# A fused two-layer kernel: two gate products as seven half-size products inside the level loop, and eleven PSUM banks moved to ScalarE

## The reference

```python
proj = h @ w_in                     # among its columns: gate_logits, 3 * 1024 wide
o_mla = causal_block_attention(...)            # 8 heads
o_gla = rms_norm(gla_chunked(...), g_gla_out) * silu(r_gla)   # 4 heads, linear attention with decay
o_mem = softmax(q_m k_m / sqrt(64)) v_m        # 4 heads over 256 memory rows
gates = sigmoid(gate_logits + b_gate).reshape(B, S, 3, D_MODEL)
y = gates[..., 0, :] * o_mla + gates[..., 1, :] * o_gla + gates[..., 2, :] * o_mem
x = x + y @ w_o
```

## Time and profile before

| | |
|---|---|
| median of 3 runs | 945.3 us (945.02 to 945.59) |
| the profiled execution, its own time | 943.98 us |
| its span | 941.6 us, so 2.4 us lie around it |
| PE busy | 926.9 us, 98% of the span |
| DVE busy | 710.9 us, 76% |
| ACT busy | 226.1 us, 24% |
| POOL busy | 37.6 us, 4% |
| chain that ended last | PE 87%, DVE 10%, ACT 1%, issue 1% |
| granted TensorE clock | full in every slice |

### The profile page before, as it was taken

The page is one execution under the profiler, slowest core; times in us unless marked ns, Lnnn a source line. Parts: engine busy times, 40 slices in busy tenths (PEclk is TensorE's granted clock), DMA queues, the critical chain, the costliest instruction groups (busy, mean ns, idle before and its releaser), DMA issues.

```text
span 941.6 us, 12480 instructions
## 1 busy us (share of the span) xinstructions
PE 926.9 (98%) x4976; PEld 584.0 (62%) x4976; DVE 710.9 (76%) x1237; ACT 226.1 (24%) x454; POOL 37.6 (4%) x58
## 2 busy tenths in 40 slices
PE   7999999999999999999999999999999999999998
PEld 5954455945555459999844459547864444469544
DVE  4875965589968787967899854888978789674676
ACT  5314422232231232332200011311103212324110
POOL 0400000000003400000000001000000000000000
PEclk9999999999999999999999999999999999999999
DMA  9753431453525624344444437522424244231721
GB/s 329 241 186 123 146 134 45 179 180 107 184 90 139 214 94 166 123 164 180 179 179 178 176 110 234 183 102 90 179 90 178 108 160 179 90 135 46 264 93 45
DMA packets 51960, 141.77 MB, mean 151 GB/s; under 512 B 4320, under 2 KB 8320, under 8 KB 51648
## 3 DMA queue, kind: packets, MB, share of 16 engines
q1 hardware_dynamic: 49152, 134.55, 40.4%
q0 software_dynamic: 2144, 5.84, 2.6%
q10 hardware_dynamic: 608, 0.61, 0.2%
HBM read 138.89 MB, written 2.10 MB: 150 GB/s over the span
## 4 chain that ended last, share of the span: by engine, by line
PE 87%; DVE 10%; ACT 1%; issue 1%; DMA 0%; DVEq 0%; ACTq 0%
PE pair L2149 30%; PE pair L2234 21%; PE pair L2230 16%; DVE arena L1079 7%; PE pair L2496 6%; PE turned L2090 3%; PE score L2496 3%; PE turned L2496 1%; PE score L2589 1%; PE score L2335 1%; PE score L2336 1%; PE score L2658 1%; PE score L2241 0%; DVE ring L1079 0%; PE turned L2576 0%
## 5 line engine op out<-in xcount | busy, mean ns | idle before, releaser
L2149 PE MATMUL pair<-ring,hT 128*128 128x512 f32 (+2 forms) x512 | 214.0, 573 | 0.9 <-ACT hT L695 0.9
L1079 DVE TENSOR_TENSOR arena<-arena 128x256 f32<-128x256 f32 (+5 forms) x326 | 194.2, 610 | 17.0 <-PE score L2496 4.1
L2149 PEld LDWEIGHTS pair<-ring,hT 128*128 128x128 f32 x512 | 95.3, 190 | 102.9 <-issue 97.7
L2234 PE MATMUL pair<-ring,arena 128*128 128x512 f32 x192 | 85.8, 594 | 0.0
L2234 PE MATMUL pair<-ring,hT 128*128 128x512 f32 x184 | 83.6, 595 | 0.1
L2234 PE MATMUL pair<-arena 128*128 128x512 f32 x176 | 79.5, 593 | 0.0
L1079 DVE TENSOR_TENSOR arena<-pair,arena 128x512 f32<-128x512 f32 x60 | 42.2, 704 | 47.2 <-PE pair L2234 26.0
L1079 DVE TENSOR_TENSOR arena<-ring 128x2048 f32<-128x2048 f32 (+1 forms) x39 | 72.3, 1854 | 2.2 <-DMA ring<-in_w_ssm_out 0.9
L2149 PE MATMUL pair<-hT,ring 128*128 128x128 f32 (+1 forms) x448 | 72.6, 322 | 0.2 <-ACT hT L691 0.2
L2149 PEld LDWEIGHTS pair<-hT,ring 128*128 128x128 f32 x448 | 64.6, 191 | 6.8 <-ACT hT L691 1.0
L2230 PE MATMUL pair<-arena 128*128 128x128 f32 x544 | 64.0, 276 | 0.0
(11 more groups left out here) (260 smaller groups left out, 1019.2 us busy)
## 6 DMA issues: line engine op xcount, KB each, us to landing
ring<-in_w_in SPq DMA_DIRECT2D x33, 2048.0 KB, 8.3
ring<-in_w_up SPq DMA_DIRECT2D x8, 2048.0 KB, 8.5
ring<-in_w_down SPq DMA_DIRECT2D x8, 2048.0 KB, 7.8
ring<-in_w_o SPq DMA_DIRECT2D x4, 2048.0 KB, 7.8
ring<-in_w_mem_kv SPq DMA_DIRECT2D x2, 2048.0 KB, 7.7
ring<-in_w_glu SPq DMA_DIRECT2D x2, 2048.0 KB, 7.8
ring<-in_w_ssm_out SPq DMA_DIRECT2D x2, 2048.0 KB, 7.8
ring<-in_w_ukv SPq DMA_DIRECT2D x1, 2048.0 KB, 7.6
```

Of the source, the lines that this page charges most:

```text
L1079: return dve.tensor_tensor(o, a, b, op)
L2149: ins = pe.matmul(o_, s, m, start=a, stop=b)
L2234: ins = pe.matmul(h[bank_], rows[:, k, :], weights[:, k, :], start=not onto and k == 0, stop=k == 3, skip_group_check=True)
```

## The change

The product for gates 4 and 5 becomes a group of seven named `GU`, spread over passes 4 to 8 of the level loop: products 1 and 5, then 2 and 7, then 3, 6 and 4. Its row sums are GT's, used again (`ROWS`). Its T1, T3 and T2 stand at the end of DVE's passes 3, 4 and 5; z and T4 at the end of pass 6. Its result is put together after the loop. Eleven banks that DVE took out of PSUM go to ACT: levels 1, 2 and 8, memory attention's four values, and the four outs. The clearing of `amat` goes from DVE to POOL, the squares of `o_gla` from DVE to ACT, and `gate_gain` from passes 4 and 5 to behind the loop. In group 2, earlier, product 7 moves ahead of the wait for `k_rows`. In the second block a one-element exponential stands ahead of the attention's loop, and `group_copy(RA, 1)` goes behind the first `exps`. POOL clears `gains`, `masks` and `m0` after `mixer_out`.

```diff
-    j = [(f"gate{i}", "w_in", C_GATE + 512 * i, 512) for i in (4, 5, 2, 3)]
+    out += halves(GT, C_GATE) + halves(GU, C_GATE + 2 * DM)
+    j = [(f"gate{i}", "w_in", C_GATE + 512 * i, 512) for i in (2, 3)]
...
@@ TensorE @@
             pe.wait_ge(sem("k_rows"), 1)      # group_multiply(2, 7) now ahead of this
...
-                elif i < 7:
-                    fill(["gate4", "gate5"], i - 4, 2)
                 else:
-                    fill(["gate4", "gate5"], i - 1, 1)
+                    for q in ((1, 5), (2, 7), (3,), (6,), (4,))[i - 4]:
+                        group_multiply(GU, q)
...
@@ VectorE, level loop @@
-                if i in (4, 5):
-                    gate_gain(i - 4)
...
-                    attend("mem", i - 2, lambda t: om_mem[:, t, EV * (i - 2):EV * (i - 1)])
+                    mark(dve.reciprocal(st[:, 360 + 2 * h:362 + 2 * h], st[:, 350 + 2 * h:352 + 2 * h]), "mem_sum")
...
-                if i == 0:
-                    link(dve.memset(amat, 0.0))
...
+                if i == 3:
+                    group_t1(GU)
+                if i == 4:
+                    group_t3(GU)
+                if i == 5:
+                    group_t2(GU)
+                if i == 6:
+                    group_z(GU)
+                    group_t4(GU)
-            for n in range(4):
-                p = scored()
-                taken_score(dve.tensor_copy(og3[:, n // 2, 512 * (n % 2):512 * (n % 2) + 512], p[:, :]))
-            gate_take(3)
...
@@ ScalarE, level loop @@
+                if i == 4:
+                    group_copy(GU, 1)
+                    group_copy(GU, 5)
...
+                if 2 <= i < EH + 2:
+                    p = ready("values", h)
+                    act.wait_ge(sem("mem_sum"), h + 1)
+                    for t in range(TT):
+                        ins = act.activation(om_mem[:, t, EV * h:EV * h + EV], p[:, EV * t:EV * t + EV], ACT.Copy,
+                                             scale=st[:, 360 + 2 * h + t:361 + 2 * h + t])
...
@@ ScalarE, second block @@
+            act.activation(st[:, 397:398], st[:, 399:400], ACT.Exp)
             for s in range(DH // 2):
-                if s == 0:
-                    group_copy(RA, 1)
...
                 for h in (2 * s, 2 * s + 1):
                     exps("dil", h, ((0, 384, 0), (384, 384, 1)))
+                    if h == 0:
+                        group_copy(RA, 1)
```

More of the change, by code:

```diff
@@ L81, with linear_units, copied @@
 SCORES = 37
-RG, MV, GT, UP = 3, 4, 5, 6
+def linear_units():
+    units = []
+    for i in range(9):
+        units += [("scores", i)] * (i < EH) + [("values", i - 2)] * (2 <= i < EH + 2) + [("level", i)]
+    return units + [("out", n) for n in range(4)]
+LINEAR = {u: 2 * MH + n for n, u in enumerate(linear_units())}
+BY_ACT = [n for u, n in LINEAR.items() if u[0] in ("values", "out") or u in (("level", 1), ("level", 2), ("level", 8))]
+def copied(*u):
+    return BY_ACT.index(LINEAR[u]) + 1
+RG, MV, GT, GU, UP = 3, 4, 5, 6, 7
 DK = UP + 4
@@ L172 @@
     "score_ready": "TensorE: banks of scores, values or states", "score_taken": "those banks out of PSUM",
+    "score_copied": "ScalarE: those of linear attention that it takes itself", "amat_zero": "GpSimd: zeros around the products within a tile",
+    "mem_sum": "heads whose sums of memory attention are inverted", "o_squared": "ScalarE: squares of a tile of linear attention's output",
     "act_step": "ScalarE's own", "dve_step": "VectorE's own", "pool_step": "GpSimd's own",
@@ L579, in _ @@
                     pool.memset(kmT[1][0:64, 0:SEQ], 0.0).then_inc(sem("key_zero"), 1)
+                    pool.wait_ge(sem("key_zero"), 4)
+                    pool.wait_ge(sem("group_product"), product_at(MV, 6))
+                    pool.memset(amat, 0.0).then_inc(sem("amat_zero"), 1)
                 if n in (2, 3):
@@ L705, in group_copy @@
                     act.wait_ge(sem("second_out"), i)
-                if i >= DK and q == 1:
+                if (i >= DK or i == GU) and q == 1:
                     act.wait_ge(sem("last_out"), i)
@@ L869, in level_exp, with ready @@
                 act.activation(dec, dec, ACT.Exp, scale=1.0 / 16.0).then_inc(sem("level_exp"), 1)
+            am3 = amat.rearrange("p (b n) -> p b n", n=P)
+            og3 = o_gla.rearrange("p (t c) -> p t c", c=DM)
+            om_mem = o_mem.rearrange("p (t c) -> p t c", c=DM)
+            def ready(*u):
+                n = LINEAR[u]
+                act.wait_ge(sem("score_ready"), n + 1)
+                return bank["score"][n % 2]
             for i in range(9):
@@ L874, in _ @@
                     level_exp(i)
+                if i == 2:
+                    p = ready("level", 1)
+                    act.wait_ge(sem("amat_zero"), 1)
+                    act.activation(am3[0:64, :, 64:128], p[0:64, :].rearrange("p (b n) -> p b n", n=64),
+                                   ACT.Copy).then_inc(sem("score_copied"), 1)
+                if i == 3:
+                    src = ready("level", 2)[:, 0:256].rearrange("p (b n) -> p b n", n=32)
+                    act.activation(am3[0:32, :, 32:64], src[0:32], ACT.Copy)
+                    act.activation(am3[64:96, :, 96:128], src[64:96], ACT.Copy).then_inc(sem("score_copied"), 1)
                 if i < 2:
                     group_copy(GT, (1, 5)[i])
+                if i == 4:
+                    group_copy(GU, 1)
+                    group_copy(GU, 5)
                 if 1 <= i <= EH:
@@ L886, in _ @@
                 if i == 8:
-                    gate_sigmoid(2)
-            gate_sigmoid(3)
+                    act.activation(across, ready("level", 8)[:, :], ACT.Copy).then_inc(sem("score_copied"), 1)
+            for n in range(4):
+                act.activation(og3[:, n // 2, 512 * (n % 2):512 * (n % 2) + 512], ready("out", n)[:, :],
+                               ACT.Copy).then_inc(sem("score_copied"), 1)
+            for t in range(TT):
+                act.wait_ge(sem("score_copied"), copied("out", 2 * t + 1))
+                act.activation((junk, qdec)[t], og3[:, t, :], ACT.Square).then_inc(sem("o_squared"), 1)
+            act.wait_ge(sem("first_out"), GU + 1)
+            act.wait_ge(sem("second_out"), GU + 1)
+            act.wait_ge(sem("last_out"), GU + 1)
+            act.activation(gate_buf, gate_buf, ACT.Sigmoid).then_inc(sem("gate_sig"), 1)
             for t in range(TT):
@@ L1522, in _ @@
                 if 2 <= i < EH + 2:
-                    attend("mem", i - 2, lambda t: om_mem[:, t, EV * (i - 2):EV * (i - 1)])
-                p = scored()
[L1526 to L1534, removed]
+                    n_score[0] += 1
+                    h = i - 2
+                    dve.wait_ge(sem("mem_exp"), h + 1)
+                    mark(dve.reciprocal(st[:, 360 + 2 * h:362 + 2 * h], st[:, 350 + 2 * h:352 + 2 * h]), "mem_sum")
+                    h, (_, _, z, v), biased = group(GT)[0], temporaries(GT), ckv[:, 0:512]
+                if i in (1, 2, 8):
+                    n_score[0] += 1
+                    if i < 8:
+                        dve.wait_ge(sem("score_ready"), LINEAR["level", i] + 1)
                 else:
+                    p = scored()
                     k = i - 3 if i else 5
@@ L1584, in _ @@
             mark(tt(o_gla, o_gla, r_gla, ALU.mult), "mixer_out")
-            gate_apply(2, 2)
-            gate_apply(3, 3)
+            dve.wait_ge(sem("score_copied"), len(BY_ACT))
+            dve.wait_ge(sem("gate_sig"), 2)
+            link(tt(o_mem, o_mem, gate_buf, ALU.mult))
             link(tt(o_mla, o_mla, o_mem, ALU.add))
@@ L2073, in _ @@
             n_unit = {"turned": 0, "score": 0}
+            by_dve = lambda n: n - sum(m < n for m in BY_ACT)
             turned_at = {}
@@ L2079, in unit @@
                 n_unit[kind] += 1
-                if n >= 2:
-                    pe.wait_ge(sem(kind + "_taken"), n - 1)
+                if kind == "score" and n - 2 in BY_ACT:
+                    pe.wait_ge(sem("score_copied"), BY_ACT.index(n - 2) + 1)
+                elif n >= 2:
+                    pe.wait_ge(sem(kind + "_taken"), by_dve(n - 1) if kind == "score" else n - 1)
                 return bank[kind][n % 2]
@@ L2307, in _ @@
             group_multiply(2, 2)
+            group_multiply(2, 7)
             pe.wait_ge(sem("k_rows"), 1)
@@ L2412, in _ @@
             pe.wait_ge(sem("amat"), 4)
+            pe.wait_ge(sem("score_copied"), copied("level", 2))
             for n in range(4):
+                if n == 2:
+                    pe.wait_ge(sem("score_copied"), copied("level", 8))
                 b = unit("score")
```

63 lines of the change are left out of this document (34 added, 29 removed).

## The result

| | before | after |
|---|---|---|
| median of the shared runs | 945.02 us (944.53 to 945.59, 5 runs) | 950.06 us (948.67 to 951.86, 5 runs) |
| profiled execution | 943.98 us, span 941.6 | 950.06 us, span 948.2 |

The ratio is 1.0054, with a 95% interval of 1.0039 to 1.0068: the change costs about 5 us. The forecast was 949.1, range 946.0 to 951.0.

What follows compares the result with a forecast made beforehand. PE was taken to bound the kernel, made to wait by DVE's sums: loop +5.5, group 2 -0.45, dilated attention -1.1, sum +3.9, rounded +3.8, so 947.8 us profiled and 949.1 for the runs, range 946.0 to 951.0.

Steps and rivals of the forecast that it cites:

- group 2: Earlier group: product 7 fills PE's 0.43 us wait for `k_rows` before the transpositions; -0.45 us, bounds 0 and -0.6.
- passes 0 to 3: Level loop's start: DVE loses clearing and copies, so PE's gaps of 1.46 and 0.69 us go; -2.15 us.
- pass 4: Level loop: product 5 waits for T1 behind DVE's chain of level 3, PE idles 2.8 us; 12.6 against 9.93, +2.7.
- pass 5: Level loop: the same chain, ending in T3, hangs on level 4, so the wait is paid again; 12.15 against 9.48, +2.7.
- passes 6 to 8: Level loop's end: product 6 waits 4.3 us for T2, product 4 for T4; 19.4 against 16.5, +2.9.
- outs, and up to `y`: Behind level 8: ACT takes level 8 instead of DVE, -0.45; DVE's lateness for `y` goes, -0.2.
- dilated attention: Second block: with the table loaded early and exponentials ahead of the copy, PE's wait for head 0 goes; -1.1 us.
- The waits: Level loop: PE idle 2.8 us each before products 5 and 7, 4.3 before 6, 2.3 before 4, ended by DVE sums.
- The clock's case: Rival: the 4.3 us wait halves PE's clock, product 6 takes 3.4 us more, 2.3 hidden; 950.2 to 953.6, chance 0.12.
- Half of it: Rival: DVE's chain is shorter than before's, each waiting pass 0.7 us less; +1.8, 947.1 us, chance 0.12.
- ScalarE was not late: Rival: ACT's added work in pass 4 delays the decays of level 5 by up to 2 us; 951, chance 0.06.
- the hidden case: Rival: PE never waits for T1 to T4, as DVE's gaps hide the sums; -7.8, 937.5 us, chance 0.09.

Runs made afterwards that it cites:

- e4: Before with only the one-element exponential ahead of the dilated attention and RA's product 1 copied behind head 0's exponentials; 942.89 us, ratio 0.9984 to before.
- e8: After with only T2, T4 and z made ahead of the level's taking, T1 and T3 left behind the levels; 943.76 us, ratio 0.9992 to before.
- e2: After with only T1 and T3 moved ahead of the level's taking, T2, z and T4 left in place; 942.94 us, ratio 0.9981 to before.
- e3: After with useless matmuls in PE's waits before products 5, 7 and 6, none before product 4; 949.35 us, ratio 1.0049 to before.
- e1: After with the same instructions, but all of DVE's sums of GU ahead of the level's taking; 936.50 us, ratio 0.9918 to before.
- e7: After with useless matmuls in all four of PE's waits, before products 5, 7, 6 and 4; 947.45 us, ratio 1.0031 to before.

## Why the prediction was right

Each step in the two profiled executions, from end to end of the same PE rows (after less before, us):

| step | forecast | measured | from |
|---|---|---|---|
| group 2 | -0.45 | -0.66 | first scores -1.15, of which -0.5 stood there already at 112 us |
| passes 0 to 3 | -2.15 | -2.28 | level 3 starts at 248.55 for 251.98, less the -1.15 |
| pass 4 | +2.7 | +2.8 | 12.7 for 9.93 |
| pass 5 | +2.7 | +4.3 | 13.8 for 9.48 |
| passes 6 to 8 | +2.9 | +2.95 | 19.46 for 16.51 |
| outs, and up to `y` | -0.65 | -0.8 | 29.4 for 30.15 |
| the loop | +5.5 | +7.0 | |
| dilated attention | -1.1 | -1.15 | |

The steps come to +5.2 where +3.9 was forecast. The -0.5 at 112 us is chance: the transposition that starts at 112.55 in before and 112.06 in after starts at 111.95 in e4, whose edit comes only near 800 us, and at 113.13 in e8, which is equal to after up to the loop. By the medians the change costs 5.04 us for 3.8.

**Passes 0 to 3.** Both gaps of the earlier trace rows went, as forecast: level 2 gained 1.5 us on the first scores, level 3 another 0.8.

**The waits.** Forecast 2.8, 2.8, 4.3 and 2.3; measured 2.52, 2.53, 4.16 and 0.39. The chain came as counted, 6.22 us from product 1's start to product 5's for 6.23; the idle time reads 0.3 shorter because the profile counts eight rows to their last end, 3.70, where I took 3.44. That the wait is paid anew in each pass is shown by e2 and e8, whose costs add. The last one shrank to 0.39 because slow product 6 filled it; at full clock, in e3, it is 2.09. The order of the lists decided the sign: e1 differs in nothing else.

**What was mis-sized.** The term "pass 5" was 1.6 us short, and this is the loop's whole error. The clock's case was priced for the 4.3 us wait alone and given 0.12; the loss came already behind 2.5 us, before product 7. At product 6 it came too and cost nothing: it was 1.7 us, not the 3.4 reckoned, and that case had 2.3 of it hidden, since product 4 waited for T4 anyway. The argument from the earlier trace rows, that no gap of before was above 1.46 us, was sound but stopped short: it left every wait between 1.46 and 4.3 open, and I treated 2.8 as safe. The reading of the earlier trace rows was weak as well: the granted clock is 1.00 from 5.24 to 9.87 us, where the first matmuls took 0.23 each, so the profile does not show a lowered clock there. The Trainium skill, "TensorE: Matmul & The Clock Gate", section on the HAM clock gate, has the clock fall back after idleness. The loop's trace agrees that it falls, here behind waits of 2.09 to 4.16 us. The page's advice on idle gaps is looser than this, and the measurement decides.

**The rivals.** "Half of it" is out: the passes are not 0.7 shorter each. ScalarE was not late: no product or level waits for it in the loop. DVE was ready for `y` 2.73 us early, for 3 forecast, so what was moved behind the loop cost nothing. With no wait for the sums, the hidden case's 937.5 is close to what e1 measured, 936.5; in after it was excluded by DVE's order alone.

**What the sum lacked.** PE's last rows come 4.65 us later than before; the profiled span is 6.6 longer. The other 1.95 us lie behind DVE's last addition, in the result's stores (5.25 us from there to the end, for 3.3). After's spans vary from 946.1 to 949.3 over five executions. The other traces point to chance: e2, e3, e7 and e8 end with the same stores, and these take 3.5 to 3.7 us there; only e1 has 5.35. What made them long in after stays open.

## What to carry to other kernels

An engine that works in order has its idle time in a place, and only work queued ahead of what it waits for can use it: 6.5 us of idleness ahead of a taking were worth nothing to a sum of 2.29 queued behind it, and moving the sums ahead, with no instruction changed, turned 5 us lost into 8.4 gained. Before giving an engine's slack to new work, follow the list from the end of the wait to that work and compare this chain with the cover of the engine that waits. Price a wait of PE at its length, and again for the clock where the row behind it is on the path.

## What the hardware showed that was not expected

- Waits of 2.09, 2.52 and 2.53 us between products could leave PE at a granted clock of 0.50 for part of the next product, whose eight rows took 5.2 to 5.4 us for 3.7. It was not each time: product 5 took 3.70 in after and 5.40 in e8 behind the same 2.52.
- Filled with useless matmuls, so that 0.17 to 0.81 us of each wait were left, the same products took 3.70 in every case profiled, and 8.6 us of useless work made the kernel about 2 us faster.
- A slow product does not always cost: product 6 lost 1.7 us in after and product 4's wait gave them back.
